# Value columns in place of query columns in the first projection stage of a hybrid diffusion trunk

## The reference, cut to what matters

```python
m = (silu(cond) @ w_ada + b_ada).reshape(6, D)           # adaLN: shift, scale, gate, twice
h = rmsnorm(x, g) * (1 + scale) + shift                  # for both streams
q, k, v = split(h @ w_qkv, 3)                            # w_qkv is 2048 x 6144: 16 heads of 128
prompt: softmax(q k^T / sqrt(128)) v                     # also returns new k and v
sample: softmax([q k^T + bias, q k_cache^T]) [v, v_cache]
y = merge_heads(o) @ w_o
```

## Time and profile before

| | |
|---|---|
| runs of the kernel | 2596.93 us median of 3 (2595.29 to 2603.23) |
| the profiled execution | 2596.33 us, span 2594.2 us |
| TensorE's mean granted clock | 0.985 of full |
| bytes moved | 634.58 MB, mean 245 GB/s |
| first stage | from 28.8 us to 141.6 us |
| attention | from 141.6 us to 453.4 us |
| output projection of attention | from 453.4 us to 553.6 us |

### The profile page before, as it was taken

The page is one execution under the profiler, slowest core; times in us unless marked ns, Lnnn a source line. Parts: engine busy times, 40 slices in busy tenths (PEclk is TensorE's granted clock), DMA queues, the critical chain, the costliest instruction groups (busy, mean ns, idle before and its releaser), DMA issues.

```text
span 2594.2 us, 38197 instructions
## 1 busy us (share of the span) xinstructions
PE 2514.9 (97%) x15138; PEld 2046.8 (79%) x15138; DVE 1361.5 (52%) x1484; ACT 1049.4 (40%) x1143; POOL 116.6 (4%) x167
## 2 busy tenths in 40 slices
PE   6899999989999999999989999999999999999998
PEld 3488888778878878878767777897787888888886
DVE  1244445466545545536555454564765465564555
ACT  3234334363333333433353355583633333343333
POOL 0021000000000000000000032200000000000000
PEclk8899999999999999999999999999999999999999
DMA  8989998758878878878885954458588655556564
GB/s 326 378 272 295 299 292 286 270 174 285 285 253 273 277 251 273 275 258 268 285 302 199 309 179 158 155 181 297 192 268 272 205 184 205 168 189 204 184 211 147
DMA packets 499594, 634.58 MB, mean 245 GB/s; under 512 B 12209, under 2 KB 384737, under 8 KB 498209
## 3 DMA queue, kind: packets, MB, share of 16 engines
q1 hardware_dynamic: 490752, 608.46, 70.4%
q0 software_dynamic: 6400, 23.31, 2.7%
q10 hardware_dynamic: 2336, 1.31, 0.2%
HBM read 623.90 MB, written 9.13 MB: 244 GB/s over the span
## 4 chain that ended last, share of the span: by engine, by line
PE 81%; DMA 10%; DVE 4%; ACT 3%; issue 1%; SPq 0%; ACTq 0%; DVEq 0%
PE PS L1229 22%; PE PS L1230 11%; PE PS L1299 10%; PE PS L1300 10%; PE PS L1301 10%; PE PS L1256 5%; DMA RAW<-in_w_mlp 3%; DMA RAW<-in_w_qkvg_gla 2%; PE PS L1238 2%; PE PS L1240 2%; PE PS L1239 2%; DVE WLO L1730 2%; ACT WHI L1491 2%; DMA RAW<-in_w_o_na 2%; DMA SCR<-in_w_ada 1%
## 5 line engine op out<-in xcount | busy, mean ns | idle before, releaser
L1730 DVE TENSOR_TENSOR WLO<-RAW,WHI 128x2048 fp32r<-128x2048 f32 (+1 forms) x386 | 876.2, 2283 | 740.7 <-ACT WHI L1491 731.7
L1491 ACT ACTIVATE WHI<-RAW 128x2048 fp32r<-128x2048 f32 (+1 forms) x386 | 729.9, 1904 | 665.1 <-DMA RAW<-in_w_mlp 453.1
L1229 PE MATMUL PS<-HM,WHI 128*128 128x512 f32 x2464 | 877.1, 400 | 1.0 <-DVE SCR L1755 0.9
L1230 PE MATMUL PS<-HM,WLO 128*128 128x256 f32 x2464 | 690.7, 280 | 0.0
L1229 PEld LDWEIGHTS PS<-HM,WHI 128*128 128x128 f32 x2464 | 462.9, 188 | 126.3 <-issue 14.7
L1230 PEld LDWEIGHTS PS<-HM,WLO 128*128 128x128 f32 x2464 | 465.2, 189 | 0.2
L1299 PE MATMUL PS<-WHI,HID 128*128 128x512 f32 x1152 | 452.4, 393 | 0.0
L1300 PE MATMUL PS<-WLO,HID 128*128 128x512 f32 x1152 | 448.6, 389 | 0.0
L1301 PE MATMUL PS<-WHI,HID 128*128 128x512 f32 x1152 | 448.2, 389 | 0.0
L1299 PEld LDWEIGHTS PS<-WHI,HID 128*128 128x128 f32 x1152 | 216.2, 188 | 56.4 <-issue 11.3
L1301 PEld LDWEIGHTS PS<-WHI,HID 128*128 128x128 f32 x1152 | 216.3, 188 | 45.3
(11 more groups left out here) (235 smaller groups left out, 1871.0 us busy)
## 6 DMA issues: line engine op xcount, KB each, us to landing
RAW<-in_w_mlp SPq DMA_DIRECT2D x256, 1024.0 KB, 5.7
ADW<-in_w_ada SPq DMA_DIRECT2D x176, 1024.0 KB, 8.8
RAW<-in_w_qkv_na SPq DMA_DIRECT2D x42, 1024.0 KB, 6.1
RAW<-in_w_qkvg_gla SPq DMA_DIRECT2D x32, 1024.0 KB, 6.6
SCR<-in_w_ada SPq DMA_DIRECT2D x16, 1024.0 KB, 12.2
RAW<-in_w_o_na SPq DMA_DIRECT2D x16, 1024.0 KB, 7.1
RAW<-in_w_qkvg_gla SPq DMA_DIRECT2D x32, 512.0 KB, 4.7
RAW<-in_w_o_gla SPq DMA_DIRECT2D x16, 1024.0 KB, 7.1
```

What stands on the lines that cost most here:

```text
L1229: mm(bank[:, 0:2 * T2], hi[:, k, cols], act[:, kc, 0:2 * T2], start=first, stop=False)
L1230: return mm(bank[:, 0:T2], lo[:, k, cols], act[:, kc, 0:T2], start=False, stop=last)
L1491: actv(WHI[:, 2 * s + u, 0:n], RAW[:, u, 0:n], ACT.Copy).then_inc(hi_done, 1)
L1730: tt(WLO[:, 2 * s + u, 0:n], RAW[:, u, 0:n], WHI[:, 2 * s + u, 0:n].bitcast(f32), ALU.subtract).then_inc(lo_done, 1)
```

## The change

The first stage computes 1536 value columns (heads 0 to 11) by tokens, in place of 768 query columns by features. A unit is now 512 rows by 512 columns, 24 matmuls of 512 columns; group j has three of them (q = 3j + v, v the column group), twelve in all, with a load of 1 MiB each. The first two units' weights of a group (one for the last group) are loaded and split early, the third after the group's second adaLN blocks and its modulation. The results stay in `FIRST_V`, in the memory that `O_HI` takes over later. Attention has 18 slabs: query and key for each of the first six pairs of heads, query, key and value for the last two. Head h is in slab h + 2. The last slab now has an adaLN unit too, and the output projection of attention computes six instead of four (`PLAN_WO0`).

```diff
-        FB = 6
-        FN = FB * P
-        FU = 2 * FN
+        FV = 3
         FIRST_ROWB, FIRST_SELB = psum[7], psum[6]
 
...
-        M_REST = M_QKV0 + FB // 2
+        M_REST = M_QKV0 + 2 * FV
         M_WO0 = M_QKV0 + 3 * D // UC
...
-        A_WO0 = A_QKV0 + M_WO0 - M_REST - 1
-        A_MLP0 = A_WO0 + NB
+        A_WO0 = A_QKV0 + M_WO0 - M_REST
+        A_MLP0 = 5 * D // UC
...
 
-        PLAN_WO, PLAN_V = ((0,), (1,), (2, 3), ()), ((0, 1), (2, 3), (4, 5), (6, 7))
+        PLAN_WO0, PLAN_WO, PLAN_V = ((0, 1), (2, 3), (4, 5), ()), ((0,), (1,), (2, 3), ()), ((0, 1), (2, 3), (4, 5), (6, 7))
...
 
-        ORDER = [(x, j) for j in range(3) for x in "KV"] + [(x, j) for j in range(3, NA_H // 2) for x in "QKV"]
+        FIRST_HEADS = 4 * FV
+        ORDER = [(x, j) for j in range(NA_H // 2) for x in ("QK" if 2 * j < FIRST_HEADS else "QKV")]
         SLABS = len(ORDER)
         LAST = SLABS - 1
         TAIL = NA_H - 2
         SLAB_OF = {kind: r for r, kind in enumerate(ORDER)}
-        HEAD_AT = {SLAB_OF["V", h // 2] + h % 2: h for h in range(TAIL)}
+        HEAD_AT = {h + 2: h for h in range(TAIL)}
...
+        FIRST_V = SCR[:, S4:S4 + 1024 * FV].rearrange("p (v s n) -> p v s n", v=FV, s=2)
...
+        def value_of(h):
+            if h < FIRST_HEADS:
+                return FIRST_V[:, h // 4, :, DH * (h % 4):DH * (h % 4) + DH]
+            return VR[h // 2 % 2][:, :, DH * (h % 2):DH * (h % 2) + DH]
...
-                pe.wait_ge(bank_free, na_evacuated("V", j))
+                pe.wait_ge(bank_free, na_evacuated("V", j) if h >= FIRST_HEADS else 4 + 2 * M_REST)
...
                     if r == LAST:
                         if q == 0:
+                            ada_rows(A_QKV0 + r)
...
                 act.wait_ge(o_copied, 4 * q + 4)
+                if q < FV:
+                    act.wait_ge(first_v_out, 16 * FV)
                 actv(O_HI[:, 4 * q:4 * q + 4, :], OQ[:, 4 * q:4 * q + 4, :], ACT.Copy).then_inc(sem("o_hi"), 1)
...
                 heads = (TAIL, TAIL + 1) if r == LAST else () if h is None else (h,)
+                if r == LAST:
+                    ada_row(A_QKV0 + r)
...
+            pool.wait_ge(bank_free, 4 + 2 * M_REST)
+            pool.wait_ge(first_out, 2)
+            for v in range(FV):
+                pool.dma_start(new_na_v[0, 0, 4 * v:4 * v + 4].rearrange("h t d -> t h d"),
+                               FIRST_V[:, v, 0, :].rearrange("p (h d) -> p h d", h=4)).then_inc(first_v_out, 16)
...
+                if h % 2 and h > FIRST_HEADS:
...
-            def load_first_weights(j):
-
-                m = j + 1
-                for u in range(2):
-                    sp.wait_ge(lo_done, m * 2 + u + 1)
-                    row = FC * j + 2 * P * u
-                    src = wq0[row:row + 2 * P, 0:FN].rearrange("(c p) n -> p c n", p=P)
-                    sp.dma_start(RAW[:, u, 0:FU].rearrange("p (c n) -> p c n", c=2), src).then_inc(raw_in[u], 16)
-
-            sp.sem_inc(raw_in[0], 16)
-            sp.sem_inc(raw_in[1], 16)
+            def load_first_weights(j, columns):
+
+                for v in columns:
+                    q = FV * j + v
+                    u, col = q % 2, 2 * D + FC * v
+                    sp.wait_ge(lo_done, M_QKV0 * 2 + q + 1)
+                    src = wq0[FC * j:FC * j + FC, col:col + FC].rearrange("(c p) n -> p c n", p=P)
+                    sp.dma_start(RAW[:, u, :].rearrange("p (c n) -> p c n", c=FG), src).then_inc(raw_in[u], 16)
+
...
             for j in range(4):
+                early = 1 if j == 3 else 2
                 load_first(2 * j)
-                load_first_weights(j)
+                load_first_weights(j, range(early))
                 load_first(2 * j + 1)
+                load_first_weights(j, range(early, FV))
...
-                if r < LAST:
-                    load_ada(A_QKV0 + r, 0, (A_QKV0 + r) * UC)
+                load_ada(A_QKV0 + r, 0, (A_QKV0 + r) * UC)
...
-                load_out(M_WO0, n, w_o_na[0], 0, range(4), plan_ada(PLAN_WO[n], A_WO0, 0))
+                load_out(M_WO0, n, w_o_na[0], 0, range(4), plan_ada(PLAN_WO0[n], A_WO0, 0))
...
-            def first_unit(j, u):
-
-                m = j + 1
+            def first_unit(q):
+
+                j, v, m, u = q // FV, q % FV, M_QKV0 + q // 2, q % 2
                 pe.wait_ge(lo_done, m * 2 + u + 3)
                 pe.wait_ge(h_ready, j + 1)
-                hi, lo = (w[:, 2 * (m % 2) + u, 0:FU].rearrange("p (c n) -> p c n", c=2) for w in (WHI, WLO))
-                for c in range(2):
-                    kc = FG * j + 2 * u + c
-                    for b in range(FB):
-                        cols = slice(P * b, P * b + P)
-                        mm(psum[b][:, 0:2 * T2], hi[:, c, cols], HM[:, kc, 0:2 * T2], start=(kc == 0), stop=False)
-                        end = mm(psum[b][:, 0:T2], lo[:, c, cols], HM[:, kc, 0:T2], start=False,
-                                 stop=(kc == KC - 1))
+                hi, lo = (w[:, 2 * (m % 2) + u, :].rearrange("p (c n) -> p c n", c=FG) for w in (WHI, WLO))
+                for b in range(2):
+                    bank = psum[2 * v + b][:, :]
+                    for k in range(FG):
+                        kc = FG * j + k
+                        xh, xl = (HM[:, kc, at:at + TOK] for at in (TOK * b, T2 + TOK * b))
+                        mm(bank, xh, hi[:, k, :], start=(kc == 0), stop=False)
+                        mm(bank, xh, lo[:, k, :], start=False, stop=False)
+                        end = mm(bank, xl, hi[:, k, :], start=False, stop=(kc == KC - 1))
                 if u == 0:
                     end.then_inc(unit0_used, 1)
                 else:
...
                     first_rows(t, v)
                     if v == 0 and t:
                         first_select(t - 1)
-                    if t % 2 and t > 1 and v == 1:
-                        first_unit(t // 2 - 1, 1)
+                    if t % 2 and t > 1 and v % 2:
+                        first_unit(FV * (t // 2 - 1) + 1 + v // 2)
                 if t % 2 == 0 and t:
-                    first_unit(t // 2 - 1, 0)
+                    first_unit(FV * (t // 2 - 1))
             first_select(7)
-            first_unit(3, 0)
-            first_unit(3, 1)
+            for v in range(FV):
+                first_unit(FV * 3 + v)
...
             for j in range(4):
+                early = 1 if j == 3 else 2
                 first_row(2 * j)
-                split_hi(j + 1, (j + 1) % 2, FU)
+                for v in range(early):
+                    first_hi(FV * j + v)
                 first_row(2 * j + 1)
                 modulate_group(0, 0, j)
-            split_hi(M_REST, 1)
+                for v in range(early, FV):
+                    first_hi(FV * j + v)
+            split_hi(M_REST, M_REST % 2)
...
-                split_lo(j + 1, (j + 1) % 2, FU)
+                early = 1 if j == 3 else 2
+                for v in range(early):
+                    first_lo(FV * j + v)
                 first_modt(2 * j + 1)
                 dve.sem_inc(xn_ready, 1)
                 modulate_sample(j, 0)
                 modulated_lo(0, j)
-            split_lo(M_REST, 1)
+                for v in range(early, FV):
+                    first_lo(FV * j + v)
+            split_lo(M_REST, M_REST % 2)
             dve.wait_ge(block_done, 4 + 2 * M_REST)
-            for b in (2, 3, 0, 1):
-                halves(OQ[:, b, :], psum[b][:, :]).then_inc(bank_free, 1)
-            for b in (4, 5):
-                halves(OQ[:, b, :], psum[b][:, :]).then_inc(first_out, 1)
+            for v in range(FV):
+                for b in range(2):
+                    ts(FIRST_V[:, v, b, :], psum[2 * v + b][:, :], 1.0, None, ALU.mult).then_inc(
+                        bank_free if v < 2 else first_out, 1)
             attention_vector(dve, split_lo, evacuate, halves)
```

More of the change, by code:

```diff
@@ L358, in outputs @@
                 pe.wait_ge(probt_ready, NA_H if h >= TAIL else h + 1)
-                pe.wait_ge(bank_free, na_evacuated("V", j))
+                pe.wait_ge(bank_free, na_evacuated("V", j) if h >= FIRST_HEADS else 4 + 2 * M_REST)
                 pe.wait_ge(vcache_in[p], 16 * (j + 1))
                 pe.wait_ge(o_copied, min(h, TAIL))
-                o, v = OUT_B[h], VR[j % 2]
-                d = slice(DH * p, DH * p + DH)
-                mm(o[:, 0:TOK], v[:, 0, d], PROBT[h][:, 0:P], start=True, stop=True)
-                mm(o[:, TOK:T2], v[:, 1, d], PROBT[h][:, P:2 * P], start=True, stop=False)
+                o, v = OUT_B[h], value_of(h)
+                mm(o[:, 0:TOK], v[:, 0, :], PROBT[h][:, 0:P], start=True, stop=True)
+                mm(o[:, TOK:T2], v[:, 1, :], PROBT[h][:, P:2 * P], start=True, stop=False)
                 return mm(o[:, TOK:T2], VCACHE[p], PROBT[h][:, 2 * P:3 * P], start=False, stop=True)
@@ L1196, in _ @@
             mm = nc.tensor.matmul
-            pe.sem_inc(unit0_used, 3)
-            pe.sem_inc(block_done, 6)
+            pe.sem_inc(unit0_used, 2 + M_QKV0)
```

(28 more changed lines are left out.)

12 lines of the change are left out of this document (6 added, 6 removed).

## The result

The changed kernel takes 2607.0 us (median of 12 runs, 2601.04 to 2609.64), the kernel before beside it 2599.7 (12 runs, 2594.94 to 2603.23). The ratio is 1.0028, 95% interval 1.0021 to 1.0036: 7.3 us slower. I had forecast 2594.4 us and no difference, with 2604 as the upper end. Of the 12.6 us between that forecast and the median, 3.4 are not the change's: the kernel before took 2599.7 here, and my sum stood on its earlier 2596.33. The change's own miss is 9.2 us.

A forecast was written before the change was run, and what follows sets the result against it. TensorE was taken to bound attention and output projection, transfers the first stage. Attention -38.7, first stage +32.9 and projection +3.9 gave -1.9 us from 2596.33: 2594.4 us, no measurable difference, range 2581 to 2604.

The forecast's parts named there:

- Attention, -38.7: Attention stage: fewer query, key and value slabs in all, no new wait, 38.7 us less.
- Output projection, +3.9: Output projection after attention: six adaLN units instead of four, 3.9 us more TensorE time; bounds +3.9 and +12.
- Step 1: Start of the first stage: with 1 MiB more ahead, rows at 58.0 us, first unit starting at 59.8.
- Steps 2 and 3: Middle of the first stage: weights of units 4 and 7 issued at 60.8 and 94.7; TensorE waits 5.4 us.
- a new wait on the load queue: First stage: a group's third unit is rounded only after modulation, so the load two units on and later adaLN loads wait.
- Step 4: Later first stage: TensorE is the bound, unit 8 stands before the last select (150.2 us), modulation done at 154.5.
- Step 5: End of the first stage: last three units end at 173.5, clearing 1.0 more, attention starts at 174.5, +32.9 us.
- only the first is waited for: Hand-over to attention: six bank clearings replace six folds, and just one of them delays TensorE.
- step 2: First stage: unit 4's weights wait for a remainder done 7.2 us after the select, landing at 66.1, not 63.4.
- The first stage absorbs more: Rival, first stage: late loads lose no time, +19 in place of 32.9, total 2580.5 us; chance 0.27.
- Slow starts: Rival, first stage: TensorE falls to 1.2 GHz at each wait for rows, 11.5 us more, total 2606; chance 0.09.
- my bound of +44: Upper bound on the first stage's growth, with slow starts after every wait.

The follow-up runs named there:

- e9: The changed kernel with units 2, 5 and 8 rounded ahead of the modulation in the first three row groups, the end left as it was: 2596.4 us.
- e6: The changed kernel with every group's third unit rounded before modulation, unit 10 too, unit 8 behind the last select, bias addition behind the bank clearings: 2588.4 us.
- e4: The changed kernel with value unit 8 behind the last select on TensorE, no longer in front of it: 2602.9 us.
- e3: The changed kernel with units 10 and 11 rounded ahead of the last modulation, not behind it: 2602.1 us.
- e10: e6 with unit 11 rounded behind the last modulation again, unit 10 still ahead of it: 2586.6 us, ratio 0.9951.

## Why the prediction was wrong

*Attention, -38.7.* Right. 37.4 were gained, after 2.5 us lost to the slow start in the first slab; PE is busy 274.1 of 274.3 us. *Output projection, +3.9.* Right: +3.7. It did not turn to its loads (295 GB/s).

*Step 1.* Right: rows at 57.20 for 58.0, U0 at 59.06.

*Steps 2 and 3, "a new wait on the load queue".* Right in kind and size: issues at 60 and 96.5 (60.8 and 94.7), next rows at 67.88 and 104.55 (68.8 and 102.7), PE idle 5.07 us (5.4). e9 and e6 show what I had not asked: the late issues, with the waits and the half clock behind them, were 10 us of the total, and nothing in the loads demands them.

*Step 4.* U8 in front of the last select, right and worth 5 us (e4). The select ended at 153.6 for 150.2. Of these 3.4 us, 1.85 were there at 104.55, and U4 took 1.3 more than its 5.5 (from 110.08 to 116.87). U2 and U5, at full clock, took 5.7 to the next rows, so 1.1 of that is a start at half clock that I had not charged. U1 had paid 0.7 in the same way (from 73.26 to 79.71, granted clock 0.50 up to 74.9), and that is part of the 1.85.

*Step 5, with "only the first is waited for".* **This is the step that failed.** The first stage grew by 40.6 us for my 32.9, beyond the 38 at which I had said I would be wrong. 3.7 of the 7.7 are step 4's lateness: the units ended at 177.25 for 173.5. The other 4.0 are the hand-over: I gave 1.0 us to the clearing, and it took 5.0. It cost 2.5 more in attention's first slab. In step 2 I had reckoned that a unit rounded behind a modulation holds its buffer and the loads behind. At the end U10 and U11 do this to attention's first slab, which leaves at 160.77, and I didn't carry the rule on. So the slab met the bias loads, which I had looked at only for the first head, and landed 11.5 and 12.3 us after its issue; its remainders stood in front of the clearing until 181.46. I priced the clearing from a row of before, where DVE had been idle 6.18 us in front of it, without asking what stands ahead of it on DVE now. e3, which rounds both units early, shows a wait of 0.88; how much of the 4.0 is the late issue and how much the slow landing stays open.

*The rivals.* "The first stage absorbs more" (+19) wasn't this kernel, but e10 comes to it: attention at 162.90, +21.3, and 12.2 us gained of its 15.8. "Slow starts" named the right sign and nearly the right time (2606) but only in part the right reason. U1 and U4 did start at half clock (0.7 and 1.1 us), and so did attention's first slab (2.5), which it does not name; U3 and U6, each after a wait of 1.7 us, started at full clock, against what it says. Of the change's miss, 4.0 us were the wait before attention, and the slab's slow start came with that wait (e3 has neither). That its time was so near is in part luck.

The range was too short above: my bound of +44 for the first stage takes in the measured +40.6 and gives 2605.5, and I cut the range at 2604.

## What to carry over

Where every block passes load, rounding and remainder through two shared buffers, a block rounded behind a dependent step stops all loads behind it. Follow that rule through to the first block of the next stage, not only within the stage. And price a hand-over by what stands ahead of it on its engine in the new order: an idle time in the old trace is the cover that may be gone. Where a load comes to leave later than it did, look at which other transfers leave at that time.
